# The order of the first tiles in a two-layer encoder trunk: x tiles asked for in a row, gates and decays of tiles 0 and 1 behind their norms, two transposes copied by ScalarE

## The reference

```python
h = _rmsnorm(x, a_norm)                                  # layer 0: gated linear attention
q, k, v, r, gl = split(h @ w_in)                         # 512 | 512 | 1024 | 1024 | 16
log_a = log_sigmoid(gl @ w_gate_up + b_gate) / 16
cum = cumsum(log_a) inside chunks of 64;  tot = cum[-1]
k_dec = k * exp(tot - cum);  state = exp(tot) * state + k_dec^T v
o = rmsnorm_per_head((q * 128**-0.5) @ state) * gn * silu(r);  x = x + o @ w_out
x = x + (silu(conv3(g)) * u) @ w_down                    # g, u = split(rmsnorm(x) @ w_up)
# layer 1: short convolution mixer, then the same MLP; a last RMS norm
```

## Time and profile before

| | us |
|---|---|
| three runs | 1466.04, 1722.61, 1762.18 |
| their median | 1722.61 |
| the profiled execution | 1466.2 |
| its span on the slowest core, from the first to the last instruction | 1464.9 |
| its span on the fastest core | 1461.2 |
| TensorE busy in that span | 1443.2 (99%) |
| VectorE, ScalarE, GpSimd busy | 813.0, 646.5, 68.8 |

### The profile page before, as it was taken

How to read it: one execution, slowest core, us unless ns; L and a number is a source line. 1 busy time by engine, 2 the same in 40 slices (tenths; PEclk the granted TensorE clock), 3 DMA queues, 4 the chain that set the end, 5 groups by cost and what they waited for, 6 DMA issues and landing times.

```text
span 1464.9 us, 20004 instructions; the slowest of 8 cores (1461.2 to 1464.9 us)
## 1 busy us (share of the span) xinstructions
PE 1443.2 (99%) x6988; PEld 659.3 (45%) x6988; DVE 813.0 (55%) x962; ACT 646.5 (44%) x1109; POOL 68.8 (5%) x103
## 2 busy tenths in 40 slices
PE   7999999999999999999999999999999999999998
PEld 3444444444444444444444444444444444444443
DVE  4247714786554455545586555576555355535567
ACT  5257656776440245024454333345442054204455
POOL 2000000001000010001000001000100001000100
PEclk9999999999999999999999999999999999999999
DMA  8941111275412312431266333167123023402314
GB/s 170 189 153 23 22 45 23 34 103 77 70 15 43 44 15 37 58 44 21 33 106 109 44 44 46 28 112 118 22 37 58 3 42 51 58 7 38 51 48 182
DMA packets 120484, 88.60 MB, mean 60 GB/s; under 512 B 61616, under 2 KB 107969, under 8 KB 120386
## 3 DMA queue, kind: packets, MB, share of 16 engines
q0 software_dynamic: 54480, 49.34, 24.5%
q1 hardware_dynamic: 65762, 37.45, 10.2%
q10 hardware_dynamic: 144, 0.52, 0.2%
HBM read 113.57 MB, written 8.39 MB: 83 GB/s over the span
## 4 chain that ended last, share of the span: by engine, by line
PE 95%; DVE 2%; ACT 1%; issue 1%; DMA 1%; ACTq 0%; DVEq 0%; SPq 0%
PE PS L520 41%; PE PS L444 28%; PE PS L602 11%; PE PS L843 11%; PE PS L901 1%; PE PS L908 1%; PE PS L943 1%; PE PS L972 0%; DMA gamma<-gam 0%; ACT xtm L336 0%; DVE PS L999 0%; PE PS L379 0%; DVE xtm L357 0%; PE PS L889 0%; DVE gl_of_u L1000 0%
## 5 line engine op out<-in xcount | busy, mean ns | idle before, releaser
L444 PE MATMUL PS<-wring_u,ffn_h_u 128*128 128x512 bf16 x1408 | 304.9, 379 | 0.0
L520 PE MATMUL PS<-xna_u,wring_u 128*128 128x512 bf16 x1344 | 292.0, 379 | 0.0
L520 PE MATMUL PS<-xnb_u,wring_u 128*128 128x512 bf16 x1344 | 292.0, 379 | 0.0
L451 DVE TENSOR_TENSOR X<-X,PS 128x512 f32<-128x512 f32 x256 | 173.4, 685 | 154.2 <-PE PS L444 154.0
L539 ACT ACTIVATE ffn_a_u<-PS,vecs_sb 128x1024 f32<-128x1024 f32 x88 | 98.0, 1113 | 262.3 <-PE PS L520 262.3
L444 PEld LDWEIGHTS PS<-wring_u,ffn_h_u 128*128 128x128 bf16 x1408 | 137.8, 98 | 166.1
L520 PEld LDWEIGHTS PS<-xnb_u,wring_u 128*128 128x128 bf16 x1344 | 131.5, 98 | 158.6
L520 PEld LDWEIGHTS PS<-xna_u,wring_u 128*128 128x128 bf16 x1344 | 131.5, 98 | 158.6
L553 ACT ACTIVATE ffn_a_u<-ffn_a_u 128x1024 f32<-128x1024 f32 x88 | 93.0, 1057 | 234.3 <-DVE ffn_a_u L549 234.2
L547 DVE SCALAR_TENSOR_TENSOR ffn_a_u<-ffn_g_u,vecs_sb,ffn_a_u 128x1024 f32<-128x1024 f32 x88 | 113.0, 1284 | 148.7 <-ACT ffn_g_u L543 78.7
L555 DVE TENSOR_TENSOR ffn_h_u<-ffn_a_u,PS 128x1024 bf16<-128x1024 f32 x88 | 107.5, 1221 | 126.1 <-ACT ffn_a_u L553 119.1
(11 more groups left out here) (112 smaller groups left out, 1065.8 us busy)
## 6 DMA issues: line engine op xcount, KB each, us to landing
wring_u<-f_w_up POOLq DMA_DIRECT2D x14, 1024.0 KB, 12.8
wring_u<-f_w_down POOLq DMA_DIRECT2D x44, 256.0 KB, 8.9
X<-x SPq DMA_DIRECT2D x15, 512.0 KB, 6.7
out<-X SPq DMA_DIRECT2D x15, 512.0 KB, 2.7
wring_u<-f_w_up POOLq DMA_DIRECT2D x8, 768.0 KB, 11.7
wring_u<-b_w_in POOLq DMA_DIRECT2D x12, 512.0 KB, 10.1
X<-a_w_out SPq DMA_DIRECT2D x8, 512.0 KB, 10.9
wr_u<-a_w_in POOLq DMA_DIRECT2D x2, 1024.0 KB, 15.3
```

Source lines behind the costliest of these rows:

```text
L444: ins = nc.tensor.matmul(self.PS[:, b, :], Y[:, k, yi * 128:(yi + 1) * 128], w[k].ap[:, n * 512:(n + 1) * 512], start=(k == 0), stop=(k == ...
L451: lambda: nc.vector.tensor_tensor(xs, xs, self.PS[:, b, :], ALU.add))
L520: ins = nc.tensor.matmul(self.PS[:, bank, :], blk.ap[:, kc, q * 128:(q + 1) * 128], self.xn(kc, hh * 8 + t * 4), start=(kc == 0), stop=(kc ...
```

## The change

- `X` tiles 1 to 5 are asked for by SyncE right behind tile 0, gamma and the constants; only tiles 6 and 7 wait, for tile 3. ScalarE's queue is gone.
- Both halves of `Wq` are asked for once tile 1 has landed.
- `busy` runs 12, 5, 5, 4, 2, 4 and 6 products (38) in place of 6, 5, 3 and 2 (16), and at other places.
- `g_decay(0)` stands behind the transposes of tile 3 and ahead of the second `g_gate`, `g_decay(1)` right behind that gate. In the kernel before they stand behind the first and the second `g_q`.
- All `g_q(0, j)` come after `turn(4)` and after six more `busy` products. `norm_a(6)` and `norm_a(7)` are issued together behind `turn(4)`, and `norm_b(6)` comes ahead of the first `g_q`.
- The transposes of tiles 5 and 6 are copied out of PSUM by ScalarE.

```diff
-        self.aq.dma(self.X[:, 1, :], xv[1], [], self.bX[1])
...
-        for i in range(2, 8):
-            if i % 2 == 0:
-                self.sp.wait(self.bX[i - 2][0].w)
+        for i in range(1, 8):
+            if i == 6:
+                self.sp.wait(self.bX[3][0].w)
             self.sp.dma(self.X[:, i, :], xv[i], [], self.bX[i])
...
+        self.pool.wait(self.bX[1][0].w)
         for h in range(2):
-            self.pool.wait(self.bX[2 * h][0].w)
             self.pool.dma(self.Wq[:, :, h * 256:(h + 1) * 256], win[:, :, h * 256:(h + 1) * 256], [], [self.bWq[h]])
...
-        self.busy(6)
+        self.busy(12)
...
         turn(0)
-        self.busy(3)
+        self.busy(5)
         turn(1)
-        self.busy(2)
         norm_a(2)
         norm_b(2)
+        self.busy(4)
         norm_a(3)
 
         self.g_gate(0, 0, 2)
         turn(2)
         norm_b(3)
+        self.busy(2)
         self.g_softplus(0)
         self.g_softplus(1)
         turn(3)
+        self.busy(4)
         norm_a(4)
-        self.g_gate(0, 2, 2)
+        self.g_decay(0)
         norm_b(4)
         self.dve.op(self.gps[1], [self.bGB[0]], lambda: nc.vector.tensor_copy(self.GB[0][:], self.gps[0]))
         self.gps = None
-        self.singles = (0, 1, 2, 3, 4, 5)
-        self.g_q(0, 0, self.dve)
-        self.g_decay(0)
+        self.g_gate(0, 2, 2)
         norm_a(5)
-        self.g_q(0, 1, self.dve)
         self.g_decay(1)
         norm_b(5)
         turn(4)
         norm_a(6)
+        norm_a(7)
+        self.busy(6)
+        self.singles = (0, 1, 2, 3, 4, 5)
+        norm_b(6)
+        self.g_q(0, 0, self.dve)
+        self.g_q(0, 1, self.dve)
+        norm_b(7)
+        turn(5, self.act)
         self.g_q(0, 2, self.dve)
-        turn(5)
-        norm_b(6)
-        norm_a(7)
+        turn(6, self.act)
+        turn(7)
         self.g_q(0, 3, self.dve)
-        norm_b(7)
-        turn(6)
-        turn(7)
         self.singles = tuple(range(8))
```

More of the change, by code:

```diff
@@ L214, in __init__ @@
         self.sp = DmaQ(nc, nc.sync, "sp", 24)
-        self.aq = DmaQ(nc, nc.scalar, "aq", 2)
         self.spo = DmaQ(nc, nc.sync, "spo", NTT + 1)
@@ L367, in norms_b, with turn_pe @@
             self.norm_b(self.normed.pop(0))
-    def turn_pe(self, st):
+    def turn_pe(self, st, eng):
         nc = self.nc
@@ L381, in turn_pe @@
         self.pe.op([self.bXTM[s], self.bident], [self.bPS[b]], tr)
-        self.copy_on(self.dve, self.XN[t // 8][:, :, t % 8 * 128:(t % 8 + 1) * 128], pt,
+        self.copy_on(eng, self.XN[t // 8][:, :, t % 8 * 128:(t % 8 + 1) * 128], pt,
                      [self.bPS[b]], [self.bXN[t]])
@@ L769, in norm_b, with turn @@
             st[i] = self.norm_b(st[i], True)
-        def turn(i):
-            self.turn_pe(st[i])
+        def turn(i, eng=self.dve):
+            self.turn_pe(st[i], eng)
         for i in range(2):
```

## The result

The changed kernel takes 1457.59 and 1458.26 us where the kernel before takes 1465.20 and 1466.04: a ratio of 0.9946, with a 95% interval of 0.9929 to 0.9964.

A forecast was written before the change was run, and what follows sets the result against it. TensorE's chain was taken to bound the kernel: `g_r` at 20.0 + 22.2 + 1.0 = 43.2 us, plus 1413.9 makes 1457.1, with 1.3 around it 1458.4, stated as 1458.5 us. The range was 1455 to 1464.5.

The forecast's parts named there:

- the sum: TensorE's order up to the first `g_r`: 20.0 + 22.2 + 1.0 = 43.2 us on the slowest core, 7.8 earlier.
- What bounds the kernel: Whole span: TensorE's chain, so the span is the start of the first `g_r` plus 1413.9 us.
- the hand-overs: Between engines ahead of `g_r`: 0.1 to 0.3 us each, some five tight, 1.0 added, bounds 0 and 2.
- Loads: Head's DMA: tiles 2 and 3 land near 9.0 and 10.3 us, tiles 4 to 7 near 12.8, 15.3, 17.8 and 20.3.
- the estimate from all bytes: Head's DMA: 4.28 MB in 18.6 us, begun at 8, end at about 26.6 us, when `Wq`'s second half lands.
- Up to tile 3's transposes: Start of the head: spread of gamma ends at 9.3 us, tile 3's transposes at 20.0 in place of 22.0.
- the near end: End of gamma's spread: the early side of 8.8 to 11.5 us, at full clock without idle time, taken as 9.3.
- From there to `g_r`: Tile 3's transposes to first `g_r`: 22.2 us of products at full clock; `norm_b(7)` tightest, ready 32.4, wanted 33.1.
- Behind `g_r`: After the head: costed at nothing; GpSimd's queue moves about 5 us, TensorE 8, so 3 us of weight slack are spent.
- A: Rival: clock still falls to 0.50 around `turn(7)`, `g_q(1)` costs 2.8 us more: 1461 to 1463 us; chance 0.23.
- B: Rival: ScalarE and VectorE pace the head's tiles, added zeros are in the way: 1464 to 1467 us; chance 0.12.
- C: Rival: `Wq`'s second half lands late beside seven tiles; landing at 43 us would give 1470; chance 0.05.

The follow-up runs named there:

- e3: Changed kernel with the PSUM copies of tiles 5 and 6 back on VectorE instead of ScalarE: 1461.18 us.
- e4: The kernel before with only the loads of the changed kernel: 1465.82 us.
- e2: Changed kernel (new order and zeros) with the loads of the kernel before: 1467.19 us.
- e5: Changed kernel with the loads of before, 16 zeros in place of 38 and all copies on VectorE, so the new order alone: 1465.39 us.
- e12: The kernel before, its order and loads kept, with 26 more products on zeros where TensorE stood idle: 1464.68 us.
- e1: Changed kernel with its 22 added zeros taken out again, new order and new loads kept: 1460.02 us.
- e6: Changed kernel without the six late zeros ahead of `g_q`, and with `norm_b(7)` ahead of the copies of q: 1456.63 us.
- e8: Changed kernel with four more products on zeros between the two halves of the spread of gamma: largest span 1458.2 us.
- e10: e6 with four of the eight folds of `a_w_out` on VectorE moved behind the product of tile 0's decays: 1457.19 us, ratio 0.994.

## Why the prediction was right, and where it was not

**The step that failed: from the sum to the range.** The prediction says of the median of 1722.61 that "no step of this sum can speak of what makes such a run", and puts this at nothing in the range. Two of the three times shown before lay 256 us and more above the profiled execution, so a range that was to hold the median of all runs had to reach there. Measured were 1457.59, 1458.26, 1618.49 and 1652.32 us, with a median of 1538.38, 74 us above the range's end of 1464.5. What makes such a run was varied in no experiment and stays open; the runs show only that one die's cores have the lower granted clock in it, and that it takes 160 to 195 us. For 1457.59 and 1458.26 the sum came out, and the rest of this section is about them.

**What bounds the kernel.** The step that carried the forecast held: the span is the start of the first `g_r` plus a constant. After, it is 1413.6 to 1414.35 us on the eight cores against 1413.9 forecast; the 0.4 on the slowest are not traced to a place.

**The sum.** The 42.65 against 43.2 is closer than its terms are: the spread ended 0.5 us later than forecast, the hand-overs cost nothing in place of 1.0, and the rest of the span took 0.4 more. That they nearly cancel is luck.

**Loads.** The second half of `Wq` was asked for at 9.5 and landed 16.7 us later, at 26.2; the estimate from all bytes was 26.6. Tile 6 landed by 20.4, when GpSimd went on with `Wr`, and not at 17.8. Most of that was late before `Wq` took a share: tile 3 was there at 12.0, when SyncE asked for tile 6, and not at 10.3. The 1.3 us a tile came from a single us at 401 GB/s; tiles 2 and 3 took 2.0 each, at 321 GB/s from 8.5 to 10.2 us and 235 from there to 12.1. Tiles 4 to 6 then took (20.4 - 12.0) / 3 = 2.8 each, between the 2.5 of the sum and the 3.2 of equal turns. The rule of the Trainium skill (DMA: Bandwidth & Descriptors, "Queues, rings and completion order"), turns by packets, taken as equal halves, fits the mean: from 12 to 20 us the two queues had 58.1% and 51.9% of engine time. In pieces of that stretch the shares went from 9.1% and 106.8% (14 to 16 us) to 75.9% and 31.0% (18 to 20.4). It changed nothing in the sum.

**Up to tile 3's transposes.** Forecast: spread ends 9.3, transposes 20.0. Measured on core 4: 7.50 + 2.26 = 9.8 and 19.98 + 0.61 = 20.6. The reason given for the near end does not hold. Core 5's spread was taken to be at full clock because the idle time ahead of it was only 1.98 us; but in the kernel before core 0 stood idle for 1.02 us and core 3 for 1.57, and their spreads took 3.75 us all the same. That the spread took 2.26 here is right by luck as far as the reason goes. And the near end by the prediction's own terms was 8.8, not 9.3.

Core 4 reaches `g_r` 2.0 us behind core 7 (42.65 - 40.69). Of this 0.7 is there when the zeros behind the spread begin (9.70 against 8.99), from slower first products; the other 1.3 is the clock's fall after that. It was not in the sum as such, but the row that the stretch was taken from the earlier trace rows had the lower clock in it too: five zeros took 2.31 us there (at 11.61 us on core 1), against 1.25 at full clock. The gain that was to be had there was thus neither forecast nor made.

**From there to `g_r`.** Forecast 22.2 of products and 1.0 of hand-overs; measured 42.65 - 20.59 = 22.1. The 1.0 was not needed: behind the decay no hand-over was open. `norm_b(7)` was named as the tightest, 0.7 us early; it ended at 33.12 and tile 7's transposes run right behind tile 6's from 33.13 on, so its margin was nothing. ScalarE's copy took 1.01 us where 1.06 was taken, and e3 shows that it did not matter on which engine it was.

**Behind `g_r`.** Costed at nothing, and measured at nothing. The slack was misjudged: the prediction moves GpSimd's queue forward by "about 5 us", although it had put `Wr` "some 8 us earlier" itself. `Wr` was asked for at 20.39 us in place of 28.40, 8.0 earlier, and none of the slack was spent; VectorE's wait for TensorE behind the folds went from 1.71 to 2.08. And the reason was given too small a place. I valued the loads by the hole that they close and by the tiles that they bring, and e4 says that this is worth 0.7 us. Their worth is that the weights behind them come 8 us earlier, for lack of which e2, e5 and e12 gained nothing (1467.19, 1465.39 and 1464.68 us). That the folds on VectorE, ahead of the product with the decays, are where a late weight strikes was not in the prediction at all: it looked at `Wr`, `Wk` and `Wv`, which TensorE reads, and not at the last load in the queue, which another engine reads ahead of something that TensorE needs.

**The rivals.** A, the clock falls in `g_q(1)`: it did not, 40 products in 8.4 us. The section of the Trainium skill on oscillation (TensorE: Matmul & The Clock Gate, "A second HAM failure mode: psum-queue depth-cycling") was not borne out here: a gap of 1.17 us ahead of tile 3's transposes, with zeros behind it, left the clock at 1.00. In e1, without zeros there, four cores fell behind a gap of 1.50 and four did not. B, the head gains nothing: refuted by 8.3 us. C, `Wq` late: its second half came at 26.2, 5.2 us ahead of its use at 31.40.

## What to carry to other kernels

A shorter head pays only as far as the next load is early enough: with the old loads, the new order, the zeros, or both of them moved `g_r` by 4.5 to 6.4 us and the end by less than 2. Before a critical stretch is shortened, follow the last transfer of the queue to the engine that reads it and to what stands behind it there. Two parts that each gain nothing alone (the loads 1465.82, the order 1465.39) were worth some 5.6 us together (1460.02 in e1, beside 1465.62 as the mean of 1465.20 and 1466.04), and the zeros, worth 1.4 at most alone (1464.68, beside a median of 1466.05), added 1.8 to that at `g_r`; so an edit tried by itself and found without effect is not yet an edit without value.

## What the runs showed of the hardware

Eight cores with one program don't see the same clock in their first 15 us: in the changed kernel twelve equal products took 4.05 us on core 0, 4.85 on core 7 and 5.28 on the six others, all started at 2.30 us. That goes with the later fall. Five of the kernels have these twelve zeros and the spread right behind them (changed, e3, e6, e8, e10), which makes 40 cores: of the 20 whose zeros took 5.04 us or less none fell to 0.50 between 10 and 15 us, and of the 20 with 5.11 or more 18 did. How many cores of a kernel fall differs without a reason in the edit: six in the changed kernel, three in e3 and two in e6, whose edits lie behind 15 us. The time is that of the slowest, so zeros that take the spread of `g_r` from 6.0 us (38.5 to 44.5 in e1) to 2.4 are worth 1.8 us although they make the fastest core later.

The granted clock that the windows show does not cover the first products. On core 4 of the changed kernel it reads 1.00 from 3 to 8 us, where twelve zeros took 5.28 us, 0.44 each, against 0.25 each at 9.70 (five in 1.25); on core 1 before it reads 1.00 from 11 to 13 us beside the five zeros in 2.31. So near the start the durations of equal products say what the clock was.

With TensorE busy to 98% of the span a granted clock of 0.99 to 1.00 can last for the whole span: all eight cores of the changed kernel's profile have 0.997 to 0.999.

Dropping ScalarE's DMA queue for tile 1 cost nothing that shows: tile 0's square started at 5.78 us on core 4 in place of 7.85 on core 1 before, tile 1's at 8.10.
